# S5 recurrence over every second time step, with the even inputs brought in through a second input matrix

## The reference, cut to what matters

```python
a_re, a_im = mag * jnp.cos(ldt_im), mag * jnp.sin(ldt_im)
...
bu_re = jnp.einsum('blgh,gph->blgp', ug, bb_re)
bu_im = jnp.einsum('blgh,gph->blgp', ug, bb_im)
...
_, _, xr, xi = lax.associative_scan(s5_combine, (ar, ai, bu_re, bu_im), axis=1)
...
y = (jnp.einsum('blgp,ghp->blgh', xr, c_re.astype(F32))
     - jnp.einsum('blgp,ghp->blgh', xi, c_im.astype(F32)))
y = y.reshape(bn, L, S5_WIDTH) + d * uf
h = jax.nn.gelu(y)
out = h * jax.nn.sigmoid(h @ w_glu)
```

## Time and profile before

| | us |
|---|---|
| median of 3 runs | 672.84 (672.66 to 672.96) |
| span of the profiled execution | 671.2 |
| TensorE busy | 661.3, 99% |
| DVE busy | 560.6, 84% |
| ACT busy | 417.7, 62% |
| POOL busy | 134.6, 20% |

### The profile page before, as it was taken

The page is one execution under the profiler, slowest core; times in us unless marked ns, Lnnn a source line. Parts: engine busy times, 40 slices in busy tenths (PEclk is TensorE's granted clock), DMA queues, the critical chain, the costliest instruction groups (busy, mean ns, idle before and its releaser), DMA issues.

```text
span 671.2 us, 13446 instructions
## 1 busy us (share of the span) xinstructions
PE 661.3 (99%) x5048; PEld 614.0 (91%) x5048; DVE 560.6 (84%) x1121; ACT 417.7 (62%) x694; POOL 134.6 (20%) x158
## 2 busy tenths in 40 slices
PE   8999999999999999999999999999999999999997
PEld 6777887989999999999977788989999999999996
DVE  6988979989998988789488998798999898884753
ACT  5776258767676666645746546786767666663343
POOL 0070420150222222200226400106022222220011
PEclk9999999999999999999999999999999999999999
DMA  8776530747674655554356463454766555556511
GB/s 326 248 261 216 201 128 1 288 107 224 212 250 155 209 178 179 202 189 153 131 181 228 159 210 130 131 204 152 204 215 195 183 181 195 173 188 193 161 56 65
DMA packets 42916, 121.82 MB, mean 181 GB/s; under 512 B 5539, under 2 KB 15171, under 8 KB 42339
## 3 DMA queue, kind: packets, MB, share of 16 engines
q1 hardware_dynamic: 40466, 115.22, 51.3%
q0 software_dynamic: 1088, 4.11, 2.5%
q10 hardware_dynamic: 1296, 1.63, 0.7%
HBM read 115.33 MB, written 5.61 MB: 180 GB/s over the span
## 4 chain that ended last, share of the span: by engine, by line
PE 90%; DVE 6%; ACT 2%; issue 1%; DMA 1%; SPq 0%; DVEq 0%; ACTq 0%
PE ps L448 21%; PE ps L449 20%; PE ps L450 20%; PE ps L441 14%; PE ps L512 2%; DVE z L1513 1%; DVE z L1521 1%; DMA z<-in_xT 1%; PE ps L460 1%; PE ps L461 1%; PE ps L462 1%; PE ps L563 1%; PE ps L575 1%; PE ps L745 1%; PE ps L797 1%
## 5 line engine op out<-in xcount | busy, mean ns | idle before, releaser
L1609 DVE TENSOR_TENSOR w_lo<-ring,w_hi 128x1024 fp32r<-128x1024 f32 x144 | 175.4, 1220 | 31.2 <-ACT w_hi L983 29.4
L448 PE MATMUL ps<-x_hi,w_hi 128*128 128x264 f32 x672 | 191.0, 284 | 1.0 <-DVE x_lo L1559 1.0
L449 PE MATMUL ps<-x_lo,w_hi 128*128 128x264 f32 x672 | 190.4, 283 | 0.0
L450 PE MATMUL ps<-x_hi,w_lo 128*128 128x264 f32 x672 | 190.3, 283 | 0.0
L983 ACT CAST w_hi<-ring 128x1024 fp32r<-128x1024 f32 x144 | 150.2, 1043 | 60.0 <-PE ps L450 58.9
L448 PEld LDWEIGHTS ps<-x_hi,w_hi 128*128 128x128 f32 x672 | 126.5, 188 | 1.9 <-issue 1.8
L449 PEld LDWEIGHTS ps<-x_lo,w_hi 128*128 128x128 f32 x672 | 126.6, 188 | 0.0
L450 PEld LDWEIGHTS ps<-x_hi,w_lo 128*128 128x128 f32 x672 | 126.0, 187 | 0.0
L441 PE MATMUL ps<-x,ring 128*128 128x264 f32 x448 | 104.7, 390 | 0.3 <-ACT x L1059 0.3
L448 PE MATMUL ps<-hff_hi,w_hi 128*128 128x264 f32 x352 | 100.0, 284 | 0.0
L450 PE MATMUL ps<-hff_hi,w_lo 128*128 128x264 f32 x352 | 99.9, 284 | 0.0
(11 more groups left out here) (364 smaller groups left out, 1148.9 us busy)
## 6 DMA issues: line engine op xcount, KB each, us to landing
ring<-in_units SPq DMA_DIRECT2D x187, 512.0 KB, 3.6
kv<-in_kpool SPq DMA_DIRECT2D x32, 128.0 KB, 2.7
kv<-in_vpool SPq DMA_DIRECT2D x32, 128.0 KB, 2.4
SR<-in_sret SPq DMA_DIRECT2D x2, 1024.0 KB, 6.2
out_rsample<-SR POOLq DMA_DIRECT2D x2, 1024.0 KB, 5.2
out_kv<-hb ACTq DMA_DIRECT2D x2, 528.0 KB, 4.5
VBC<-v_rows POOLq DMA_DIRECT2D x8, 128.0 KB, 3.9
out_y<-x SPq DMA_DIRECT2D x3, 264.0 KB, 2.0
```

The source lines that it names most:

```text
L448: mm(out, wh, hi, start=start, stop=False)
L449: mm(out, wh, lo, start=False, stop=False)
L450: return mm(out, wl, hi, start=False, stop=stop)
L1609: E.did(tt(w_lo[:, slot], ring[:, ring_slot(L * UNITS + i)], w_hi[:, slot].bitcast(F32), ALU.subtract), "w_lo")
```

## The change

The recurrence runs over the 128 odd positions with the squared factor. The input of a half is stored parted: first the even positions, then the odd ones and samples. `s5_b` is one call for a half, with the old matrix on the odd positions and a second one, `s5ba` = aB, on the even ones, summed in the bank. aB is made by `s5_b_step` (six DVE operations of 128x256), four transposes (`s5_turn_b`) and an ACT copy (`s5_b_back`). For the readout of even positions `s5_c` uses C a (`cfa`, made by `s5_readout_step`, six DVE operations) and C B (`K0`, made by `s5_near` with 16 small matmuls and four ACT copies, `s5_near_back`). Tables, rotations and scans have half their length. B comes in a second time, transposed (`s5bt`, 256 KB a layer). For the second layer these new steps stand among the down products of the first.

```diff
-AT = [{"b00": 3, "b01": 4, "ss": 6, "sc": 7, "tab": 8, "vbt": 8, "b10": 9, "b11": 11, "c0": 11, "logs": 10, "srg": 12,
-       "tails": 16, "c1": 17, "vt": 17, "glu": 18, "inner": 18, "kt": 18, "vb": 16, "values": 18, "sv": 18, "rsq": 18,
+AT = [{"tb": 5, "b0": 6, "ss": 6, "k0": 7, "sc": 7, "tab": 6, "vbt": 8, "b1": 8, "c0": 10, "logs": 9, "srg": 10,
+       "c1": 13, "tails": 13, "glu": 15, "inner": 15, "kt": 15, "vt": 16, "vb": 16, "values": 16, "sv": 16, "rsq": 16,
...
+S5_PE = [4, 6]
+S5_BACK = [15, 20]
+S5_BANK = [3, 7]
...
+            def s5_turn_b(L):
+
+                need(pe, "cf", L, 1)
+                bank = claim(S5_BANK[L], "s5tev", L, 1)
+                for c in range(2):
+                    for hf in range(2):
+                        at = (2 * c + hf) * P
+                        ins = nc.tensor.transpose(bank[:, at:at + P],
+                                                  bpow[:, c, hf * HJ:(hf + 1) * HJ].rearrange("p a b -> p (a b)"), C["ident"])
+                E.did(ins, "s5t")
+
+            def s5_near(L):
+
+                need(pe, "cf", L, 3)
+                bank = claim(S5_BANK[L], "s5tev", L, 1 + HJ)
+                for hf in range(2):
+                    for c in range(2):
+                        for jj in range(HJ):
+                            ins = mm(bank[32 * jj:32 * jj + 32, 32 * hf:32 * hf + 32], s5bt[:, c, hf * HJ + jj],
+                                     cf[:, c, hf * HJ + jj], start=(c == 0), stop=(c == 1), tile_position=(0, 32 * jj))
+                E.did(ins, "s5t")
+
+            def s5_b(L, hf):
+                pe.wait_ge(S("ld_s5b"), 32 * (L + 1))
+                need(pe, "s5tev", L, 1)
                 needr(pe, "rawh", 2 * L, hf + 1)
...
+                banks = [claim(4 + jj, "buev", L, hf + 1) for jj in range(HJ)]
+                for c in range(2):
+                    for jj in range(HJ):
+                        r = slice(32 * jj, 32 * jj + 32)
+                        mm(banks[jj][:, c * BC:(c + 1) * BC], s5b[r, c, hf * P:(hf + 1) * P], hb[r, U + hf, SQ:T],
+                           start=True, stop=False)
+                    for jj in range(HJ):
+                        r = slice(32 * jj, 32 * jj + 32)
+                        ins = mm(banks[jj][:, c * BC + NS // 2:c * BC + NS // 2 + SQ], s5ba[r, c, hf * P:(hf + 1) * P],
+                                 hb[r, U + hf, 0:SQ], start=False, stop=True)
...
             def s5_c(L, hf):
                 need(pe, "s5x", L, hf + 1)
                 if hf == 0:
-                    need(pe, "cf", L, 2)
+                    need(pe, "cf", L, 4)
                     need(pe, "cneg", L, 1)
+                    need(pe, "s5tev", L, 1 + HJ)
                 bank = claim(2, "yd", L, hf + 1)
+                mm(bank[:, 0:SQ], K0[:, hf], hb[:, U + hf, 0:SQ], start=True, stop=False)
...
+                        mm(bank[32 * jj:32 * jj + 32, second:second + SQ], cf[:, c, hf * HJ + jj], X[:, jj],
+                           start=False, stop=False, tile_position=(0, 32 * jj))
...
+                        mm(bank[32 * jj:32 * jj + 32, 1:SQ], cfa[:, c, hf * HJ + jj], X[:, jj, 0:SQ - 1],
+                           start=False, stop=False, tile_position=(0, 32 * jj))
...
-                        if L == 0:
-                            open_gates(L)
...
-                    if L > 0 and i == 17:
+                    if i == (18, 17)[L]:
                         open_gates(L)
...
+                        if d == S5_BACK[1]:
+                            s5_near_back(L + 1)
                             s5_tables(L + 1, 0)
...
             def s5_pre(L, hf):
 
                 TC, TS = tabs[hf]
+                BR, BI = (bri[hf][:, c, :, tm] for c in range(2))
                 need(dve, "tab", L, 2 * hf + 2)
-                need(dve, "buev", L, 2 * hf + 1)
-                E.did(tt(P2[:, :, tm], TC, BR[:, :, tm], ALU.mult))
-                E.did(tt(P4[:, :, tm], TS, BR[:, :, tm], ALU.mult))
-                need(dve, "buev", L, 2 * hf + 2)
+                need(dve, "buev", L, hf + 1)
                 E.settle()
                 if hf == 1:
                     need(dve, "s5y", L, 1)
...
+                    m = mag2[:, hf * HJ + jj:hf * HJ + jj + 1].to_broadcast([P, SQ])
+                    E.did(nc.vector.tensor_tensor_scan(BR[:, jj], m, P1[:, jj], 0.0, ALU.mult, ALU.add))
+                    E.did(nc.vector.tensor_tensor_scan(BI[:, jj], m, P3[:, jj], 0.0, ALU.mult, ALU.add))
```

More of the change, by code:

```diff
@@ L29 @@
 SEQ, NS = 256, 8
+SQ = SEQ // 2
+BC = SQ + NS
 T = SEQ + NS
@@ L769, in sb_tails @@
                 mm(bank[:, 0:32], C["ones"], s1, start=False, stop=True)
[L770 removed]
+                E.did(mm(bank[:, 32:64], C["tri"], s1, start=True, stop=True), "sbs")
             def sb_values(L):
@@ L834, in _ @@
                               (lambda k: need(pe, "x", L, k + 1)) if i == RAW else None)
[L835 to L838, removed]
+                    if L == 0 and i == at_["tb"]:
+                        pe.wait_ge(S("ld_cst"), 16)
+                        s5_turn_b(L)
+                    if i == at_["b0"]:
+                        s5_b(L, 0)
                     if i == at_["ss"]:
                         sb_sample_scores(L)
+                    if L == 0 and i == at_["k0"]:
+                        s5_near(L)
                     if i == at_["sc"]:
-                        if L == 0:
-                            pe.wait_ge(S("ld_cst"), 16)
                         sb_sample_turn(L)
                         sb_scores(L)
+                    if i == at_["b1"]:
+                        s5_b(L, 1)
                     if i == at_["c0"]:
@@ L947, in _ @@
                         ln_shift(2 * L + 2)
+                    if L + 1 < DEPTH and m == S5_PE[0]:
+                        s5_turn_b(L + 1)
+                    if L + 1 < DEPTH and m == S5_PE[1]:
+                        s5_near(L + 1)
             ln_sums(2 * DEPTH)
@@ L1137, in s5_params @@
                     act.wait_ge(S("s5par_v"), 3 * L + 2)
+                    f(mag2[:], disc[:, 1], ACT.Exp, scale=2.0)
                     E.did(f(mag[:], disc[:, 1], ACT.Exp), "s5par_a")
@@ L1155, in neg_c, with s5_evac, s5_b_back, s5_near_back @@
                 E.did(nc.scalar.mul(s5c[:, 1], s5c[:, 1], -1.0), "cneg")
[L1157 to L1162, removed]
+            def s5_evac(L, hf):
+                need(act, "bu", L, hf + 1)
+                E.did(nc.scalar.copy(bri[hf][:], ps[:, 4:8, 0:2 * BC].rearrange("p a (c k) -> p c a k", c=2)), "buev")
+            def s5_b_back(L):
+                need(act, "s5t", L, 1)
+                E.did(nc.scalar.copy(s5ba[:], ps[:, S5_BANK[L]].rearrange("p (c k) -> p c k", c=2)), "s5tev")
+            def s5_near_back(L):
+                need(act, "s5t", L, 2)
+                need(act, "qz0", L, 1)
+                for jj in range(HJ):
+                    r = slice(32 * jj, 32 * jj + 32)
+                    E.did(nc.scalar.copy(K0[r, :, r], ps[r, S5_BANK[L], 0:64].rearrange("p (h k) -> p h k", h=2)), "s5tev")
             def sb_first(L):
```

245 lines of the change are left out of this document (154 added, 91 removed).

## The result

The changed kernel takes 685.1 us (median of 4, 684.23 to 687.15) against 672.9 before: 1.0182 times the time, 95% interval 1.0166 to 1.0199. I had forecast 680.1 and at most 682.8. The direction and the place of most of the loss were right, the size was not.

A forecast was written before the change was run, and what follows sets the result against it. TensorE's ordered matmuls plus its few waits were taken to bound the kernel. Terms 1.3 + 2.1 + 1.7 + 0.7 + 2.5 + 0.4 - 1.4 = +7.3 on 672.84 gave 680.1 us, range 674.8 to 682.8.

The forecast's parts named there:

- s5_b, four halves: TensorE input products: one call per half at 1.28 us instead of two at 1.70; -1.7 us over both layers.
- s5_c, four halves: TensorE readout products: an added full-array product with K0 in each half, +0.22 us each; +0.9 us.
- s5_turn_b, s5_near: New TensorE work in both layers: four transposes, +1.0 us, and 16 small column-tile matmuls, +1.1 us.
- readout wait, first layer: TensorE before s5_c(1): DVE's 12.8 us chain exceeds the 10.7 us cover of three tiles; +2.1 us.
- readout wait, second layer: TensorE before s5_c(1): DVE's 12.8 us chain against 11.1 us cover of three tiles and vb transposes; +1.7 us.
- second mean square: TensorE's second root-mean-square product, first layer, waits for square_b behind the gates block on ACT; +2.5 us.
- waits removed: TensorE waits at the s5_b evacuation, L441, L632 and L460 disappear; -1.4 us.
- The wait for the second readout: Largest term: TensorE waits before s5_c(1) for DVE's halved chain, +2.1 us first layer, +1.7 second.
- The gates: ACT's 3.47 us table-load and SiLU block behind tile 18, ahead of square_b, delays the second mean square; +2.5 us.
- The layer boundary: ACT's copies for second-layer s5_near delay tables, cast and scaled columns; mostly slack, 0 to 1.5, taken as +0.4 us.
- The wait for K0: First layer: sb_sample_turn waits for four ACT copies to empty bank 3 after s5_near; +0.7 us.
- the rivals: Four alternatives: smaller waits, 675.6 to 678.1 us (chance 0.25); longer, 682.1 to 684.5 (0.12); no change, 672.7 (0.06); faster (0.05).

The follow-up runs named there:

- e6: Changed kernel with second-layer vb transposes back behind tile 8 and ACT's early weight casts back behind the sigmoid; 683.14 us against 685.1.
- e3: Changed kernel with the second readout one tile later in both layers and sb_third ahead of s5_skip(1) on DVE; 679.03 us against 685.1.
- e4: Kernel before with only the first layer's open_gates moved right in front of square_b; 678.09 us against 673.09, ratio 1.0078.
- e5: Changed kernel with s5_near of the second layer one down output tile earlier, behind m = 5; 684.19 us against 685.1.
- e7: Changed kernel with the first layer's s5_turn_b and s5_near in PSUM bank 2 instead of 3; 685.02 us against 685.1.
- e9: Changed kernel with the first layer's sb_second ahead of s5_pre(1) on DVE and the logarithms behind tile 8 instead of 9; 683.01 us against 685.1.
- e1: Changed kernel with the first layer's gates opened one tile earlier, behind tile 17; 681.01 us against 685.1.
- e8: Changed kernel with e1, e3, e5, e6 and e7 together; 672.36 us against 672.67 of the kernel before, ratio 0.9993.
- e2: Changed kernel with six overwritten products on TensorE in front of the first layer's second mean square; 684.19 us against 685.1.
- e10: Changed kernel with e2's six overwritten products plus five in front of the first layer's second readout; 683.58 us against 685.1.

## Why the prediction was wrong

By its own steps, predicted and measured in the profiled executions:

| step | predicted us | measured us |
|---|---|---|
| s5_b, four halves | -1.7 | -1.8 (with 3.56 for the tile ahead a call is 1.21 to 1.32, against 1.70 for two calls) |
| s5_c, four halves | +0.9 | +1.3 (60.44 to 61.87 is 1.43, against 1.10) |
| s5_turn_b, s5_near | +2.1 | +1.9 (in the down products 0.36 and 0.48, in the first layer 0.44, and about 0.6) |
| readout wait, first layer | +2.1 | +2.1 |
| readout wait, second layer | +1.7 | +1.0 |
| vb transposes | not seen | +0.5 |
| K0 copies | +0.7 | +1.1 |
| second mean square | +2.5 | +2.8 |
| half clock behind it | not seen | +1.7 |
| layer boundary | +0.4 | +1.0 |
| sigmoid and key transposes | not seen | +1.2 |
| waits removed | -1.4 | -1.4 |
| sum | +7.3 | +11.4, where the span grew by 11.2 |

The steps "The wait for the second readout" and "The gates" were right in mechanism, and near in size. In the second layer the wait of 0.5 at the vb transposes took the place of part of the readout's 1.7; e6 shows that they trade, so both together, 1.5, are what I had as one; in e6, without the wait of 0.5, the readout's is 1.7 as forecast. I had counted these transposes as cover of 0.44 us, without asking for what they wait: moved behind tile 7, they follow directly on the tile that they transpose, and ACT must copy it out first.

Four things were wrong, in order of size.

1. "The gates" priced the wait at its own length and put the clock behind it at nothing. The wait can also cost the clock: 1.7 us in the profiled execution. Of the seven profiled executions with this idle wait (the changed kernel, e3, e4, e5, e6, e7, e9) six have a spell of half clock at it, and e6 has none; where the wait is gone (e1, e8) or filled (e2, e10) no spell is there. Of the six with the idle 2.12 us at the first layer's readout (the changed kernel, e1, e2, e5, e6, e7) four have a spell behind it. So the fall goes with long idle waits, shown over the kernels together; what decides in one execution whether it comes stays open. The median rose 12.2 us where the profiled span rose 11.2, and the profiled execution was the fastest of the four and had the highest mean clock, 0.997 against 0.994 to 0.996.
2. The sigmoid's delay (1.2) was not on my list. The changed order puts ACT's cast for tile 16 (with its wait for the weights, 0.99) ahead of the sigmoid; I took the earlier casts only as the removal of a wait (L460) and didn't ask what stood behind them on ACT.
3. "The layer boundary" was mis-sized, 0.4 for 1.0. The bounds, 0 to 1.5, held it.
4. "The wait for K0" was mis-sized, 0.7 for 1.1: ACT's four copies take 0.88, and the two handovers a further 0.2 together.

Of the rivals, none came: the chain of DVE was 12.75 us for 12.8, scans did shrink to 0.32, and a table load is followed at once by the next instruction (112.88, 1.28 long; the SiLU at 114.17). So the drain that the Trainium skill gives for such a switch (ScalarE: Activation LUTs, What ACT_TABLE_LOAD costs) does not show here. On small DVE operations the spacing, 0.61, was what counted, not the 0.69 of the row's own duration. That 0.69 is also what the Trainium skill (VectorE: DVE Perf Modes, The TRN2 errata) gives for one operation of this length.

## What to carry to other kernels

Where one engine is full, halving the work of another is worth only the waits that it shortens; look for these first, and here there were 1.4 us of them against as much added matmul time. A schedule that is compressed around the new, shorter chain must leave the chain its length: from each step back to the one that releases it, in its own engine's order, table loads and casts included. And where the change makes TensorE idle for long (here 2.1 us and more), leave room in the range for the clock: of 14 such waits in the profiled executions ten cost about 1.7 us more than their length, one about 3, and three nothing.

## What the runs showed of the hardware

Apart from the last 2 us of the span, the granted clock of TensorE fell to 0.50 eleven times in the profiled executions, always at an idle wait of 2.06 to 3.2 us: behind or at the second mean square (2.84 and 3.2 us) in the changed kernel, e3, e4, e5, e7 and e9, behind the readout (2.12 us) in e2, e5, e6 and e7, and behind the sigmoid (2.06 us) in e10. It did not fall behind 2.84 us in e6, nor behind 2.12 us in the changed kernel and e1, nor at the wait of 1.7 us in e6's second layer. The spells last 3.4 us, and 6.8 in e9. They begin between 0.7 us before the work resumes (e9; in e3 0.1 before) and 1.5 us after (e2, e6). In the profiled executions of e8 and of the kernel before, whose longest wait is 1.2 us, no window of 10 us up to 660 is below 1.00. Executions of e1 fall into two groups 1.7 us apart (680.07 and 680.23, 681.79 and 682.06), with mean clocks of 1.000 and 0.997; 3.4 us at half clock lower the mean over this span by 0.0025. A scan of 128 elements starts 0.32 us after the last, one of 256 0.59. The 16 products of s5_near (column tiles of 32, 32 columns each) take 0.48 us in the down products and about 0.6 behind an in-projection tile.
